# State-space scan on one core: the order of its row products, turns and first copies

## The reference, cut to what matters

```python
xbc = jax.nn.silu(causal_dwconv(xbc, conv_w, conv_b))      # 1536 channels, 4 taps
dt  = jax.nn.softplus(dt_raw + dt_bias);  A = -jnp.exp(a_log)
Acs = jnp.cumsum(Adt, axis=-1)                             # within a chunk of 128 tokens
seg = Acs[..., :, None] - Acs[..., None, :]
Ldec = jnp.where(causal, jnp.exp(jnp.where(causal, seg, 0.0)), 0.0)
CB = jnp.einsum('bclgn,bcsgn->bgcls', Cc, Bc)
y_diag = jnp.einsum('bgcls,bgjcls,bcsgjp->bclgjp', CB, Ldec, Xdt)
states = jnp.einsum('bclgn,bgjcl,bclgjp->bcgjpn', Bc, decay_states, Xdt)
_, prev = lax.scan(step, init, (states, chunk_decay))      # one chunk after the other
y_off = jnp.einsum('bclgn,bcgjpn,bgjcl->bclgjp', Cc, prev, jnp.exp(Acs))
y = y_diag + y_off + xs * d_skip;  y = y * jax.nn.silu(z)
```

## Time and profile before

| | us |
|---|---|
| median of 3 runs | 1686.3 |
| lowest and highest run | 1679.79, 1690.04 |
| the profiled execution's own time | 1682.23 |
| its span (first to last instruction) | 1680.5 |

### The profile page before, as it was taken

The page is one execution under the profiler, slowest core; times in us unless marked ns, Lnnn a source line. Parts: engine busy times, 40 slices in busy tenths (PEclk is TensorE's granted clock), DMA queues, the critical chain, the costliest instruction groups (busy, mean ns, idle before and its releaser), DMA issues.

```text
span 1680.5 us, 29124 instructions
## 1 busy us (share of the span) xinstructions
PE 1582.7 (94%) x10740; PEld 1369.2 (81%) x10740; DVE 1037.6 (62%) x1561; ACT 514.7 (31%) x1093; POOL 893.0 (53%) x838
## 2 busy tenths in 40 slices
PE   6999997999999999998988999999997999999997
PEld 4888865897888888988887878788995988998885
DVE  4599826469737877885767877776325666565001
ACT  4311012121146753333225555554214110111111
POOL 1455420566773408663236654434471777777774
PEclk8999999999999999999999999999998999999999
DMA  8346321323210003221111111111231232333322
GB/s 313 114 134 205 126 69 31 108 69 95 76 38 2 27 1 88 76 78 49 38 51 39 39 51 51 38 50 51 64 89 38 77 98 87 95 92 101 96 85 93
DMA packets 208568, 131.08 MB, mean 78 GB/s; under 512 B 5294, under 2 KB 194254, under 8 KB 208350
## 3 DMA queue, kind: packets, MB, share of 16 engines
q1 hardware_dynamic: 208478, 129.82, 25.9%
HBM read 127.71 MB, written 2.10 MB: 77 GB/s over the span
## 4 chain that ended last, share of the span: by engine, by line
PE 83%; DVE 10%; ACT 3%; issue 2%; DMA 1%; SPq 0%; DVEq 0%; ACTq 0%
PE ps L2264 21%; PE ps L2265 20%; PE ps L2267 20%; PE ps L2583 2%; PE ps L2609 2%; PE ps L2901 2%; DVE sb_sum L2092 1%; PE ps L2570 1%; DMA ada_first<-in_ada_w 1%; PE ps L2808 1%; PE ps L2561 1%; PE ps L2876 1%; PE ps L2712 1%; PE ps L2470 1%; PE ps L2811 1%
## 5 line engine op out<-in xcount | busy, mean ns | idle before, releaser
L749 POOL TENSOR_SCALAR w_hi<-raw 128x512 fp32r<-128x512 f32 x370 | 273.8, 740 | 682.6 <-PE ps L2267 230.8
L751 POOL TENSOR_TENSOR w_lo<-raw,w_hi 128x512 fp32r<-128x512 f32 x370 | 525.5, 1420 | 30.9
L2264 PE MATMUL ps<-xn_hi,w_hi 128*128 128x264 f32 (+1 forms) x800 | 234.9, 314 | 12.3 <-ACT xbc L1193 5.5
L2264 PE MATMUL ps<-op_hi,w_hi 128*128 128x512 f32 x608 | 215.5, 354 | 1.8 <-DVE op_lo L1489 1.7
L2265 PE MATMUL ps<-xn_lo,w_hi 128*128 128x264 f32 (+1 forms) x800 | 213.7, 287 | 0.0
L2265 PE MATMUL ps<-op_lo,w_hi 128*128 128x512 f32 x608 | 204.9, 354 | 0.0
L2267 PE MATMUL ps<-op_hi,w_lo 128*128 128x512 f32 x608 | 177.9, 352 | 0.0
L2264 PEld LDWEIGHTS ps<-xn_hi,w_hi 128*128 128x128 f32 x800 | 153.0, 191 | 26.4 <-issue 12.6
L2264 PE MATMUL ps<-u_hi,w_hi 128*128 128x258 f32 (+1 forms) x528 | 163.2, 323 | 5.7 <-DVE u_lo L2151 5.4
L2267 PE MATMUL ps<-xn_hi,w_lo 128*128 128x264 f32 (+1 forms) x800 | 164.0, 287 | 0.0
L2265 PE MATMUL ps<-u_lo,w_hi 128*128 128x258 f32 (+1 forms) x528 | 162.9, 322 | 0.0
(11 more groups left out here) (440 smaller groups left out, 3199.1 us busy)
## 6 DMA issues: line engine op xcount, KB each, us to landing
raw<-in_w_in SPq DMA_DIRECT2D x45, 512.0 KB, 3.8
raw<-in_w_up SPq DMA_DIRECT2D x44, 512.0 KB, 3.7
ada_ring<-in_ada_w SPq DMA_DIRECT2D x14, 1024.0 KB, 5.2
raw<-in_w_in_ab SPq DMA_DIRECT2D x20, 512.0 KB, 5.7
raw<-in_w_in_c SPq DMA_DIRECT2D x20, 512.0 KB, 3.7
ada_first<-in_ada_w SPq DMA_DIRECT2D x4, 2048.0 KB, 17.0
raw<-in_w_out SPq DMA_DIRECT2D x16, 512.0 KB, 3.6
raw<-in_w_down SPq DMA_DIRECT2D x16, 512.0 KB, 3.6
```

The source lines that it names most:

```text
L749: steps(nc.gpsimd.tensor_scalar(hi, r, 1.0, 0.0, ALU.mult, ALU.add))
L751: nc.gpsimd.tensor_tensor(lo, r, hi.bitcast(F32), ALU.subtract)\
L2264: mm(o[:, 512 * b:512 * b + n], w_h[:, k, :], hi[:, k0 + k, c0:c0 + n], start=a, stop=False)
```

## The change

Nothing is computed in another way; four pieces of order change.

- In the loop over convolution tiles, the silu of the tile two places back stands ahead of ScalarE's wait for the slab instead of behind it.
- The first chunk's copy is made in two parts: the small dt rows and ten tiles as soon as ten silus are done, the last two tiles after the last silu. VectorE raises `dt_ready` earlier, so that the first copy need not wait for the end of the convolution.
- On TensorE, `rows(1)` stands after piece 5 of the first slab instead of after piece 8 (in the last chunk after 5 instead of 4), and the turns of the next chunk, with their wait, ahead of the second slab instead of behind it.
- On ScalarE, the `take_z` of the first slab stands behind the second exponential instead of ahead of it.

```diff
--- before.py
+++ after.py
@@ -1182,9 +1182,9 @@
 
             def xbc_pair(i):
                 for j in range(2):
+                    conv_silu(2 * i + j - 2, j)
+
                     act.wait_ge(s["slab_done"], g0 + j + 1 + 2 * i)
-                    conv_silu(2 * i + j - 2, j)
-
                     act.wait_ge(s["conv_done"], 4 * i + 2 * j - 3)
                     nc.scalar.activation(two(conv[:, j, :]), halves(gemm_ps[(b0 + j) % 2]), ACT.Identity,
                                          scale=cols[:, 1, bass.ds(2 * i + (j + XC * 3), 1)],
@@ -1206,8 +1206,16 @@
                 conv_silu(j, j)
             with act.Fori(2, XC // 2) as i:
                 xbc_pair(i)
-            for j in range(2):
-                conv_silu(XC - 2 + j, j)
+            conv_silu(XC - 2, 0)
+
+            act.wait_ge(s["dt_ready"], 1)
+            nc.scalar.copy(dt_t[0:16, :], xbc[0:16, XC, 0:P]).then_inc(s["chunk_in"], 1)
+            act.wait_ge(s["conv_done"], 2 * XC - 4)
+            steps(nc.scalar.copy(xst[0][:, 0:XC - 2, :], xbc[:, 0:XC - 2, 0:P]))
+            conv_silu(XC - 1, 1)
+            act.wait_ge(s["conv_done"], 2 * XC - 2)
+            steps.wait()
+            nc.scalar.copy(xst[0][:, XC - 2:XC, :], xbc[:, XC - 2:XC, 0:P]).then_inc(s["chunk_in"], 1)
 
             g0z = SLAB0["z"]
 
@@ -1238,8 +1246,7 @@
             def chunk_in(i, j):
 
 
-                if not (isinstance(i, int) and i + j == 0):
-                    act.wait_ge(s["ssd_used"], max(j, 1) + 2 * i)
+                act.wait_ge(s["ssd_used"], max(j, 1) + 2 * i)
                 back = bass.ds(i * 2 * P + j * P, P)
                 nc.scalar.copy(xst[j % 2][:, :, :], xbc[:, 0:XC, back]).then_inc(s["chunk_in"], 1)
                 nc.scalar.copy(dt_t[0:16, :], xbc[0:16, XC, back]).then_inc(s["chunk_in"], 1)
@@ -1252,13 +1259,14 @@
                                          ACT.Exp).then_inc(s["chunk_e"], 1)
                     if g == 0 and more:
                         chunk_in(i, j + 1)
-                        take_z(2 * (2 * i + j) + 1)
                     elif g == 0:
 
                         act.wait_ge(s["ssd_used"], NT)
                         clear_other(0)
                         take(0, 0, g0 + 1)
-                if not more:
+                if more:
+                    take_z(2 * (2 * i + j) + 1)
+                else:
                     take(0, 1, g0 + 2)
                 act.wait_ge(s["dec_in"], j + 1 + 2 * i)
                 nc.scalar.activation(dec[:, :], acs[:, :], ACT.Exp).then_inc(s["dec_ready"], 1)
@@ -1270,8 +1278,6 @@
                     take_z(2 * (2 * i + j) + 2)
 
 
-            act.wait_ge(s["dt_ready"], 1)
-            chunk_in(0, 0)
             nc.scalar.preload_act_table_set("natural_log_exp_and_others")
             take_z(0)
             for t in range(NT):
@@ -1901,6 +1907,7 @@
                 steps(nc.vector.tensor_tensor(xbc[:, n, PAD:TP], xbc[:, n, PAD:TP], PRE_ROWS, ALU.mult))
             steps(nc.vector.memset(xbc[:, :, 0:PAD], 0.0))
             steps.wait()
+            dve.sem_inc(s["dt_ready"], 1)
 
             taps = 4
 
@@ -1953,7 +1960,6 @@
                     convolve(i, j)
             steps.wait()
             dve.wait_ge(s["conv_done"], 2 * XC - 2)
-            dve.sem_inc(s["dt_ready"], 1)
 
             dve.sem_inc(s["ssd_used"], 1)
             H = 16
@@ -2731,19 +2737,17 @@
                     ins = mm(pair_ps[1][:, S + P + c * P:S + 2 * P + c * P], xst_t[:, KC + c, :],
                              xst_t[:, KC + 2 + c, :], start=True, stop=True)
                 ins.then_inc(s["chunk_sums"], 1)
-                beside(2 if more else 0, KC if more else KC // 2)
+                beside(2 if more else 0, 5)
 
                 pe.wait_ge(s["seg_sub"], 2 * j + 1 + 4 * i)
                 rows(1)
-                if not more:
-                    beside(KC // 2, KC)
+                beside(5, KC)
                 if not more:
                     first_chunks(-1, 0, KC)
                 else:
-                    z_chunks(t, 2, 0, KC)
-
                     pe.wait_ge(s["seg_sub"], 2 * j + 2 + 4 * i)
                     chunk_turn(i, j + 1)
+                    z_chunks(t, 2, 0, KC)
                 pe.wait_ge(s["ssd_operands"], j + 1 + 2 * i)
                 for h in range(H):
                     o = pair_ps[0][HEAD * (h % 2):HEAD * (h % 2) + HEAD, (h // 2) * P:(h // 2 + 1) * P]
```

## The result

| | before | after |
|---|---|---|
| median of 13 runs each | 1685.84 us | 1675.32 us |
| lowest and highest run | 1679.79, 1692.98 | 1670.87, 1678.58 |
| the profiled execution's own time, span | 1682.23, 1680.5 | 1675.60, 1673.8 |

The ratio is 0.9937, with an interval of 0.9919 to 0.9954: 0.6% less. The forecast was 1675.9 us. The two profiled executions differ by 6.6 us, the medians by 10.5.

A forecast was written before the change was run, and what follows sets the result against it. TensorE, busy 1582.7 of 1680.5 us, bounds the kernel. Terms 6.5 - 0.2 + 0.8 + 3.3 = 10.4 us, taken from the median 1686.3, gave 1675.9 us, range 1667 to 1685.

The forecast's parts named there:

- The bound, and what the edits reach: Whole kernel: TensorE's work plus waits bounds it; edits reach only waits, one barrier pause and slow clock, some 15 us.
- Row products earlier, turns ahead of the slab: Chunks 0 to 3: the 2.1 us wait ahead of output products goes, 1.63 us a chunk, 6.5 us in four.
- The new wait: Ahead of the turns, chunks 0 to 3: TensorE waits 0.46 us for the second subtraction.
- The spare of the operand: Chunks 0 to 3: TensorE reaches the output products 0.6 us after the decayed operand is ready.
- The last chunk: Row products one piece later there make the operand late: a loss of 0.2 us ahead of the output products.
- The barrier: After the last convolution slab: silu ahead of its wait lets the tap start earlier, 0.8 us less TensorE idle.
- The copy in two parts: First chunk's copy, ahead of the turns: taken as 0, between 0 and 0.8 us if the slab ran at full clock.
- The clock: Output products of chunks 2 and 3: both slow stretches taken as gone, 3.3 us, bounds 0 and 3.3.
- the waits go, the clock does not come back: Rival: slow stretches fall at other pauses, such as the barrier or behind the scan; gain 7.1, 1679.2 us; chance 0.22.
- The new position waits: Rival: row products or turns wait at their new places in chunks 0 to 3; 1681 to 1683 us; chance 0.09.
- Slower by the clock: Rival: shifted work behind the scan gains five more slow stretches of 1.65 each; 1687.5 us; chance 0.07.
- The first rival's rule: Only idle gaps clearly longer than this stage's bring slow clock, so the slow stretches have another cause and need not go.

The follow-up runs named there:

- the changed kernel's second profile: The changed kernel itself, unedited, run again on another chip: median 1675.40 us, ratio 0.9941 to the kernel before.
- barrier alone: Kernel before with only silu ahead of the slab wait, the first copy in two parts and early dt_ready: 1688.45 us, ratio 1.0013 to before.
- old wait back: Changed kernel with VectorE computing the decayed operand 2.5 times more in chunks 0 to 3, so TensorE waits again: 1687.45 us, ratio 1.0012 to the kernel before.
- the scan's edits alone: Kernel before with only the new places of row products, turns and slab copy: 1678.78 us, ratio 0.9956 to before.
- the run with piece 4: Changed kernel with the row products after piece 4 instead of 5 in chunks 0 to 3: 1681.09 us in one run.

## Why the prediction was right

The time and the waits came as forecast, and by the mechanism that was forecast. The clock's part came out at its size, but by another way than was forecast: that was luck in good part.

**The bound, and what the edits reach.** Held. TensorE's busy time did not change (1582.7 and 1583.1 us), its idle time fell, and the waits' part of the result is close to what the loop's timeline gave.

**Row products earlier, turns ahead of the slab.** The mechanism held at every step: no wait at the row products, the exponential right behind them, a wait ahead of the turns put down to the subtraction, none ahead of the output products. The forecast was 1.63 a chunk; the period fell from 25.17 to 23.68, 1.49. The term was too large by 0.14. The new wait was 0.42, against 0.46 forecast; the sign given for it, 0.3 to 0.6, was not what the rows read, since they show 0.24 to 0.26 of idle. But the second slab now takes 6.05 up to the output products, where it took 5.93 up to the turns, and the three pieces behind the row products take 2.27, where 2.22 was reckoned. Four chunks gave 6.0 instead of 6.5. The spare of the operand was forecast as 0.6 and was 0.7.

**The last chunk.** A loss of 0.2 was forecast; with the old place the same way took 6.01 instead of 6.20, 0.19. It does not show as a wait on the row of the first output product, as the prediction said it would. The chunk lost more in another place, at TensorE's pause ahead of its first pieces, which the prediction did not look at. Before, two pauses stood there, 1.22 and 1.36, and the pieces behind them ran at full clock. After, these were 0.26 and 2.21, and the pieces took 1.5 longer. The same pieces in the changed kernel's second profile, behind a like pause, ran at full clock (3.72 from the first piece to the row products, where the first profile has 5.26):

```profile
870.42 0.36 PE L2270 MATMUL ps<-xn_hi,w_hi 128*128 128x264 f32 x1 [2.23 <-ACT q_even L1234]
...
874.14 1.95 PE L2718 MATMUL ps<-tri,adt 128*128 128x128 f32 x16
```

The long pause (1.72 to 2.23) stands in all ten profiles in which chunk 3's output products ran at full clock, and seven of these have the slow pieces behind it. In the three with slow output products there (before, barrier alone, old wait back) the pauses are 1.22 and 1.36, and the pieces run at full clock.

**The barrier.** The forecast was 0.8 less pause, the traces say 0.70. For the clock of the slab I counted nothing and gave a bound of 1.4: it did come back whole in all eleven profiles with a pause of 1.60, and was lost again one pause later in ten of them: the first row products, behind 2.03 to 2.28, took 2.6 to 3.6 instead of 2.05. The cost there is 1.6, so on balance the zero was right, by two errors that cancel. The copy in two parts was put at 0 for the slow slab and up to 0.8 for the fast one; the slab was fast, and its worth is some 0.4.

**The clock** was forecast as 3.3. No single pair of profiles can tell: the one at hand gave 1.5 inside the stage (4.7 given, 3.2 taken) and took 2.6 behind it. The runs can. Every run has a span and a mean clock. Over all kernels with five or more runs, a line of common slope says that 0.001 of mean clock goes with 1.13 us. The kernel before has a mean clock of 0.9772 (60 runs), the changed one 0.9804, 0.9795 and 0.9812 (13, 11 and 6 runs): 2.5 to 4.5 us, the three together 3.4. At equal clock (0.978) the mean spans are 1683.5 and 1675.5 to 1675.6, 7.9 apart, where the waits were forecast as 7.1 and measured as 6.7. The agreement of the sum is better than that of its parts.

The way there was not the one forecast. The prediction took the scan's two slow stretches as gone and counted nothing elsewhere. With the scan's edits alone the clock gave 1.1, not 3.3, and the barrier's edits alone took 1.7; only together do they give 3.4, and no run says why. Two slow stretches as the base was one profile's count, too: the three profiles with the waits have two, four and two.

So of the rivals, "the waits go, the clock does not come back" (1679.2) describes the profiled pair, and the kernel with the scan's edits alone (1678.78), but not the changed kernel's medians: all three lie below 1675.5. "The new position waits" is what the run with piece 4 shows, one piece away. "Slower by the clock" did not come, though its mechanism is there: behind the scan the pair lost 2.6. The prediction also said that over 1% slower would need ten new slow stretches; with the 7.1 of the waits gone it would need about fifteen (16.9 + 7.1 = 24.0, at 1.65 each), which only makes that chance smaller.

The link of pause and slow clock is now on more rows. Of the twelve pauses of 2.07 to 2.46 ahead of output products (kernel before, barrier alone, old wait back), eight were followed by a slow stretch of 1.6 to 1.7. In the ten profiles without such a pause, none of the 40 chunks has one there. The old wait put back into the changed kernel brought two of them back. So a slow stretch in this place comes with the pause ahead of it only; what decides which of them brings one is not shown. The first rival's rule, the Trainium skill's "TensorE: Matmul & The Clock Gate", section "HAM oscillation — how this bites in real kernels", which warns only of longer gaps, would have left these stretches where they were; the traces disagree with it here.

What stays open: why one and the same pause is followed by slow clock in one chunk and not in the next, and whether the slow row products and the slow pieces of the last chunk are the stretches that the barrier's slab and the output products lost, or others. After a slow slab (kernel before, scan alone) the first row products were fast; after a fast slab they were slow in ten of eleven profiles. That is a pattern, no cause; no run here varied it by itself.

## What to carry to other kernels

When one engine is bound and waits at the end of a loop for a chain that starts at its own output, move the start of that chain forward until its own input becomes late, then fill the place behind it with work that does not depend on the chain; two engines' timelines of one period give the gain to 0.15 us of 1.6. Count a pause of about 2 us on TensorE at more than its length: here eight of twelve ahead of the output products cost 1.6 to 1.7 more. Take that as a mean over runs, since one profile had two of its four slow and another all four. And look at the next pause behind the one that is removed: in seven of ten profiles a slow stretch stood there. Judge an edit worth under 0.5% by its period and waits in the trace: two kernels that differ by 0.7 us of pause came out 2.7 us apart in the median, the wrong way, with an interval that holds no difference.

## What the runs showed that was not expected

A recurring pause of 2.1 to 2.5 us, 25 us apart, was followed by slow clock in two, four and two of four cases in three profiles. The 60 runs of the kernel before spread over 15 us (1679.5 to 1694.3), and 13 on one chip beside the kernel with only the scan's edits, whose 12 runs spread over 3.6 (1676.95 to 1680.57). The 13 runs of the changed kernel spread over 8 (1670.87 to 1678.58), with the pause at the barrier shorter. So less of a pause went with more spread here; that a slow stretch comes and goes elsewhere would explain it, but no run shows it.

A slow stretch that is removed may turn up behind the next pause: the barrier's slab gained 1.4 (5.95 instead of 7.35), and the row products 9.5 us later lost 1.6 behind a pause of 2.18 that both kernels have. Where the slab had run slow (kernel before, scan alone), full clock followed that pause.
